# Expert lanes in units of 32 rows, x first in the weights' queue, SSD decays on ScalarE

## The reference

```python
for l in range(DEPTH):
    sh_m, sc_m, g_m, sh_f, sc_f, g_f = split(silu(c) @ w_ada[l] + b_ada[l], 6)
    h = rms_norm(x, norm_gain[l, 0]) * (1 + sc_m) + sh_m
    if l % 2 == 0: y = concat(rwkv7(h @ w_in_even ...), gla(h @ w_in_even ...))
    else:          y = concat(hgrn2(h @ w_in_odd ...), ssd(h @ w_in_odd ...))
    x = x + g_m * (y @ w_out[l])
    h = rms_norm(x, norm_gain[l, 1]) * (1 + sc_f) + sh_f
    x = x + g_f * grouped_moe(h, ...)        # 16 experts, top 2 of one group of 4
return rms_norm(x, final_gain)
```

## Time and profile before

| | us |
|---|---|
| median of 3 runs | 1642.72 |
| lowest, highest | 1634.35, 1645.2 |
| the profiled execution | 1631.18 |
| its span | 1629.4 |

### The profile page before, as it was taken

The page is one execution under the profiler, slowest core; times in us unless marked ns, Lnnn a source line. Parts: engine busy times, 40 slices in busy tenths (PEclk is TensorE's granted clock), DMA queues, the critical chain, the costliest instruction groups (busy, mean ns, idle before and its releaser), DMA issues.

```text
span 1629.4 us, 22551 instructions
## 1 busy us (share of the span) xinstructions
PE 1434.7 (88%) x9837; PEld 743.0 (46%) x9837; DVE 674.6 (41%) x1044; ACT 306.5 (19%) x500; POOL 71.5 (4%) x199
## 2 busy tenths in 40 slices
PE   5999999967878797899999859969998789999992
PEld 3445565536666545433333344535654353333331
DVE  2114334235677316432333235785643543332334
ACT  2121211123342103100000042221112400000002
POOL 7000000000000000000000010000000000000001
PEclk9899999987999898999999979989999989999997
DMA  9686674031000007999997761201100599989884
GB/s 343 219 293 198 207 242 146 1 116 41 3 3 32 24 0 279 404 424 375 353 426 294 273 244 52 78 26 52 52 0 0 233 374 400 386 339 421 335 348 168
DMA packets 91215, 334.17 MB, mean 205 GB/s; under 512 B 6521, under 2 KB 37485, under 8 KB 74733
## 3 DMA queue, kind: packets, MB, share of 16 engines
q1 hardware_dynamic: 76880, 287.94, 46.4%
q10 hardware_dynamic: 8476, 23.82, 3.7%
q0 software_dynamic: 5760, 20.97, 3.4%
HBM read 309.65 MB, written 23.07 MB: 204 GB/s over the span
## 4 chain that ended last, share of the span: by engine, by line
PE 74%; DVE 14%; DMA 6%; ACT 4%; issue 2%; POOL 0%; DVEq 0%; SPq 0%; ACTq 0%; POOLq 0%
PE banks L1736 18%; PE banks L1284 14%; PE banks L1758 10%; PE banks L1656 5%; DVE work L1872 4%; PE banks L1325 4%; PE banks L1273 3%; PE banks L1220 3%; DMA work<-in_w_down_dram 2%; PE banks L1640 2%; PE banks L1719 1%; DVE work L1878 1%; DMA work<-h_rows,idx_tok 1%; PE banks L1450 1%; DMA ring<-in_w_ada_dram 1%
## 5 line engine op out<-in xcount | busy, mean ns | idle before, releaser
L1284 PE MATMUL banks<-h_features,ring 128*128 128x512 f32 (+1 forms) x656 | 291.3, 599 | 5.6 <-ACT h_features L897 4.0
L1736 PE MATMUL banks<-ring,work 128*64 128x512 f32 x672 | 231.3, 600 | 2.3 <-issue 2.3
L1736 PE MATMUL banks<-work 128*64 128x512 f32 x512 | 212.2, 595 | 0.0
L1284 PEld LDWEIGHTS banks<-h_features,ring 128*128 128x128 f32 (+1 forms) x656 | 121.4, 189 | 158.0 <-issue 154.3
L1872 DVE TENSOR_TENSOR work<-work,banks 128x256 f32<-128x256 f32 (+2 forms) x88 | 47.7, 564 | 190.6 <-PE banks L1736 144.7
L1758 PE MATMUL banks<-work 128*64 128x512 f32 x320 | 112.7, 593 | 0.0
L1872 DVE TENSOR_TENSOR work<-work 128x512 f32<-128x512 f32 (+9 forms) x202 | 100.2, 496 | 14.5 <-ACT work L1092 3.6
L1736 PEld LDWEIGHTS banks<-ring,work 128*64 128x64 f32 x672 | 72.1, 138 | 68.6 <-issue 63.9
L1758 PE MATMUL banks<-ring,work 128*64 128x512 f32 x256 | 98.4, 592 | 0.0
L1736 PE MATMUL banks<-h_features,work 128*64 128x512 f32 x192 | 89.5, 614 | 2.2 <-ACT work L1143 2.2
L1656 PE MATMUL banks<-y_features,ring 128*128 128x512 f32 x192 | 84.6, 603 | 6.4 <-DVE small L2404 6.4
(11 more groups left out here) (360 smaller groups left out, 1822.5 us busy)
## 6 DMA issues: line engine op xcount, KB each, us to landing
ring<-in_w_up_dram SPq DMA_DIRECT2D x16, 2048.0 KB, 13.0
y_features<-in_w_ada_dram SPq DMA_DIRECT2D x28, 1024.0 KB, 5.7
work<-in_w_down_dram SPq DMA_DIRECT2D x14, 2048.0 KB, 13.4
ring<-in_w_gate_dram SPq DMA_DIRECT2D x12, 2048.0 KB, 12.2
work<-in_w_up_dram SPq DMA_DIRECT2D x10, 2048.0 KB, 13.3
work<-in_w_gate_dram SPq DMA_DIRECT2D x10, 2048.0 KB, 12.7
ring<-in_w_ada_dram SPq DMA_DIRECT2D x8, 2048.0 KB, 12.2
h_features<-in_w_gate_dram SPq DMA_DIRECT2D x8, 2048.0 KB, 9.4
```

What stands on the lines that cost most here:

```text
L1284: ins = mm(PS[0:w, b, :], lhsT=W[:, k, c0:c0 + w], rhs=h[:, k, :], start=(k == 0), stop=(k == KD - 1))
L1736: ins = mm(PS[rows, bank, :], lhsT=xt[:, k, rows], rhs=ws[lane][:, k, :], start=(k == 0), stop=(k == KD - 1))
```

## The change

Five things:

- **Lanes in units of 32 rows.** `LANES` now counts units of 32 rows, two to a round, and `ROUNDS` is 10. A run may begin or end in the middle of a round: in lane 1 at unit 3 and at unit 11, so rounds 1 and 5 have two experts in that lane. `weights` then returns three parts (rows, weights) instead of two, and `lanes_up` and `lanes_down` loop over them. `choose` takes four numbers for each place (first block, blocks, rows skipped at the front, rows skipped at the end) and puts the rows of an expert accordingly.
- **Start.** SyncE issues x first, then `w_ada[0]` rows in four pairs of row blocks, 2048 columns wide ("first"), the fourth into `y_features`. `first_sums` accumulates them in one bank, quarter g of the columns in part g; one copy and one turn (`first_turn`) replace four.
- **SSD.** The eight subtractions go to ScalarE, as Relu of (cum of the row - value) from PSUM, and the following Exp has scale -1. So does the copy of xs. The decay to the end of the tile is read from the decays themselves (`Es[:, :, P - 1:P]`) instead of being formed apart. `ssd_tile` runs for tiles 0 and 1 before `ssd_scores(0)`.
- **Zeroing.** `lqp` and `lgate` are zeroed for layer 1 by GpSimd after the first layer's combination; VectorE's memsets there go.
- **Order.** The ring order is one entry shorter.

```diff
-LANES = ([1, 1, 1, 1, 2, 1, 2, 2], [2, 3, 2, 1, 2, 1])
-ROUNDS = 11
+QUARTER_ROWS = 32
+LANES = ([2, 2, 6, 2, 2, 4, 2], [3, 3, 2, 3, 3, 4, 2])
+ROUNDS = 10
...
+def place_numbers(u, n, lane):
+    lead = QUARTER_ROWS * (u % 2)
+    skip = -(lead + QUARTER_ROWS * n) % HALF_ROWS
+    return 2 * (u // 2) + lane, (lead + QUARTER_ROWS * n + skip) // HALF_ROWS, lead, skip
...
-    plan = [("ada", 0, i) for i in range(4)]
+    plan = [("first", 0, i) for i in range(3)]
...
+            sp.dma_start(work[:, 0:4096].rearrange("p (a d) -> p a d", d=D),
+                         A["x"][0].rearrange("(a p) d -> p a d", p=P)).then_inc(sem("x_loaded"), 16)
             for n in RING_ORDER:
                 load(n)
+                if n == 2:
+                    sp.dma_start(first_place(3), first_src(3)).then_inc(sem("half_loaded0"), 16)
...
+                if l == 0:
+                    pool.wait_ge(sem("comb_added"), NT)
+                    pool.memset(lqp.rearrange("p a b -> p (a b)"), 0.0).then_inc(sem("pool_const"), 1)
+                    pool.memset(lgate.rearrange("p a b -> p (a b)"), 0.0).then_inc(sem("pool_const"), 1)
...
-                act.wait_ge(sem("seg_diff"), t + 1)
-                act.activation(Es2[t % 2], Es2[t % 2], ACT.Exp).then_inc(sem("seg_exp"), 1)
+                act.wait_ge(sem("score_ready"), 3 * NT + t + 1)
+                for hd in range(8):
+                    ins = act.activation(Es2[t % 2][:, hd, :], PS[:, b + hd // 4, (hd % 4) * P:(hd % 4 + 1) * P], ACT.Relu,
+                                         scale=-1.0, bias=cumc[:, t, hd:hd + 1])
+                link(ins)
+                act.activation(Es2[t % 2], Es2[t % 2], ACT.Exp, scale=-1.0).then_inc(sem("seg_exp"), 1)
...
+            def first_sums(i):
...
+                for k in range(2):
+                    for g in range(4):
+                        ins = mm(PS[32 * g:32 * g + 32, 5, :], lhsT=cond[:, 2 * i + k:2 * i + k + 1].to_broadcast([P, 32]),
+                                 rhs=w[:, k, 512 * g:512 * g + 512], start=(i + k == 0), stop=(i + k == 4))
...
+                    parts = []
                     for lane in range(2):
...
+                        places = [place_at(2 * r + i, lane) for i in range(2)]
+                        width = HALF_ROWS if places[0] == places[1] else QUARTER_ROWS
+                        for i, place in enumerate(places[0:HALF_ROWS // width]):
+                            home = home_of(part, place)
+                            if PLACES[place][0] // 2 == r:
+                                pe.wait_ge(loaded[l][home], 16 * (loads_before(l, home) + loads_of(home, (place, part))))
+                            p0 = HALF_ROWS * lane + QUARTER_ROWS * i
+                            parts.append((slice(p0, p0 + width), home_w(home, part)))
+                    return parts
...
                     for k in ks:
-                        for lane in range(2):
-                            rows = slice(64 * lane, 64 * lane + 64)
-                            ins = mm(PS[rows, bank, :], lhsT=xt[:, k, rows], rhs=ws[lane][:, k, :], start=(k == 0),
+                        for rows, w in ws:
+                            ins = mm(PS[rows, bank, :], lhsT=xt[:, k, rows], rhs=w[:, k, :], start=(k == 0),
                                      stop=(k == KD - 1))
...
+            first_sums(1)
             norm(0)
+            first_sums(2)
+            first_sums(3)
+            first_turn()
             projections(0)
...
                 elif step == LOGS:
-                    signal(dve.memset(f2(lqp), 0.0), "log_pre")
+                    dve.wait_ge(sem("pool_const"), 3)
...
-                for hd in range(8):
-                    link(tsc(Es[:, hd, :], PS[:, b + hd // 4, (hd % 4) * P:(hd % 4 + 1) * P],
-                             cumc[:, t, hd:hd + 1], ALU.subtract, 0.0, ALU.min))
...
-                pk = picked2.rearrange("p k (e n) -> p k e n", n=E)
-                link(tt(pk, bc(at_place, 2, 1), bc(place_of, E, 2), ALU.mult))
+                pk = picked4.rearrange("p k (e n) -> p k e n", n=E)
+                link(tt(pk, bc(at_place, 4, 1), bc(place_of, E, 2), ALU.mult))
                 link(dve.tensor_reduce(begin_runs, pk, AX_X, ALU.add))
...
+                link(tt(late, rank, bc(cap_rows, NT, 1), ALU.is_ge))
+                link(tt(placed, late, bc(skip, NT, 1), ALU.mult))
+                link(tt(placed, placed, rank, ALU.add))
+                link(tt(placed, placed, bc(lead, NT, 1), ALU.add))
```

More of the change, by code:

```diff
@@ L63, in load_plan @@
     at = {phase: i for i, phase in enumerate(phase_order())}
-    loads = sorted((place > 1, at[part, r], lane, at[part, r + n - 1], place, part)
-                   for place, (r, n, lane) in enumerate(places) if r < ROUNDS for part in range(3))
+    loads = sorted((place > 1, at[part, u // 2], lane, at[part, (u + n - 1) // 2], place, part)
+                   for place, (u, n, lane) in enumerate(places) if u < 2 * ROUNDS for part in range(3))
     held = [-1] * 8
@@ L97, in chunk_plan @@
     plan += [("in", 0, i) for i in range(4, 7)]
-    plan += [None, None] + [("out", 0, i) for i in range(2)]
+    plan += [None, None, None] + [("out", 0, i) for i in range(2)]
     plan += [("in", 1, i) for i in range(6)] + [("out", 1, i) for i in range(2)]
@@ L223, in trunk @@
         quarter_ends = small(1)
+        quarter_rows = small(4)
         idx_tok = sb("idx_tok", MAX_BLOCKS + 2, I32)
@@ L438, in trunk, with place_at, home_of, last_home @@
         gathered = [[sem(f"l{l}_{j}_rows_gathered") for j in ("even", "odd")] for l in range(DEPTH)]
-        def home_of(part, r, lane):
-            place = [p for p, run in enumerate(PLACES) if run[2] == lane and run[0] <= r < run[0] + run[1]][0]
+        def place_at(u, lane):
+            return [p for p, run in enumerate(PLACES) if run[2] == lane and run[0] <= u < run[0] + run[1]][0]
+        def home_of(part, place):
             return [home for p, which, home, _ in LOADS if p == place and which == part][0]
+        def last_home(part, lane):
+            return home_of(part, place_at(2 * ROUNDS - 1, lane))
         def loads_of(home, last=None):
@@ L448, in loads_of @@
             return len(users) if last is None else users.index(last) + 1
-        IN_LOOP = [home_of(part, ROUNDS - 1, lane) for part in range(3) for lane in range(2)]
+        IN_LOOP = [last_home(part, lane) for part in range(3) for lane in range(2)]
+        assert len(set(IN_LOOP)) == 6
         loaded = [[sem(f"l{l}_home{i}_loaded" if i in IN_LOOP else f"home{i}_loaded") for i in range(8)]
@@ L561, in units_at @@
             return [("half", HALVES_AT.index((n, i)))] if (n, i) in HALVES_AT else []
-        UNITS = [("piece", i) for i in range(4)] + [unit for n in range(27) for i in range(2) for unit in units_at(n, i)]
-        FIRST_UNITS = 4
-        assert len(UNITS) == 10 + HALVES
+        UNITS = [("first", 0)] + [unit for n in range(27) for i in range(2) for unit in units_at(n, i)]
+        FIRST_UNITS = 1
+        assert len(UNITS) == 7 + HALVES
         def unit_width(unit):
-            return 512 if unit[0] == "piece" else 256
+            return 256 if unit[0] == "half" else 512
         def unit_weights(unit):
@@ L623, in load @@
                     sp.wait_ge(sem("rows_cleared"), 16)
-                if n >= RING and PLAN[n - RING] is not None:
-                    kind, l, i = PLAN[n - RING]
-                    if kind == "ada":
+                earlier = [key for key in PLAN[n % RING:n:RING] if key is not None]
+                if earlier:
+                    kind, l, i = earlier[-1]
+                    if kind == "first":
+                        sp.wait_ge(sem("unit_summed"), i + 1)
+                    elif kind == "ada":
                         sp.wait_ge(sem("unit_summed"), unit_done("piece", i))
@@ L691, in _ @@
                         for lane in range(2):
-                            home = home_of(part, ROUNDS - 1, lane)
+                            home = last_home(part, lane)
                             src = ws[part][l][bass.ds(es[lane], 1)]
@@ L1790, in again @@
                     def again(part):
-                        for home in last[part]:
+                        homes_of = [last_home(part, lane) for lane in range(2)]
+                        for home in homes_of:
                             pe.wait_ge(loaded[l][home], (it + (loads_of(home) + 1)) * 16)
-                        return [home_w(home, part) for home in last[part]]
+                        return [(slice(HALF_ROWS * lane, HALF_ROWS * lane + HALF_ROWS), home_w(home, part))
+                                for lane, home in enumerate(homes_of)]
                     pe.wait_ge(sem(f"l{l}_xt_copied"), it + (ROUNDS + 1))
@@ L2612, in _ @@
             link(dve.memset(lsum, 0.0))
+            parameters()
+            norm(0)
             copy_unit(0)
-            parameters()
-            copy_unit(1)
-            norm(0)
-            for u in range(2, FIRST_UNITS):
```

(1 more changed line is left out.)

174 lines of the change are left out of this document (92 added, 82 removed).

## The result

| | before | after |
|---|---|---|
| median of 4 runs, us | 1643.96 | 1689.01 |
| lowest, highest | 1634.35, 1648.37 | 1686.48, 1692.4 |
| span of the profiled execution | 1629.4 | 1690.6 |

The changed kernel is slower: the ratio of the times is 1.0283, with a 95% interval from 1.0234 to 1.0333. The forecast was 1585.5 with a range from 1564 to 1612; the time lies on the second rival's 1689. Four of the forecast's terms are in the trace nevertheless, so the stages come first.

What follows compares the result with a forecast made beforehand. TensorE was taken as the bound, its long work the expert rounds, with waits at the start and in SSD. Terms -45.2 + 2 + 4 + 2 - 8 - 12 gave -57 us: 1585.5 against the median, range 1564 to 1612.

Steps and rivals of the forecast that it cites:

- the second rival: Mixed steps in rounds 1 and 5 of both layers: widths don't overlap, +46 us in all, 1689 us; chance 0.20.
- Mixed rounds: Rounds 1 and 5 of each layer, 96 steps of three parts: a third part on its own columns nearly free, +2 us.
- the upper end: Mixed rounds, bound from above: 64 to 32 counts as a width change, a step takes 2.00 us for 0.86, +109 us.
- The test at the prediction's end: Expert stages: a mixed round longer than 37 us would above all show the forecast wrong.
- Rounds: Expert stages: 10 static rounds a layer instead of 11, one dynamic pass kept, 2 x 22.6 = -45.2 us.
- Weights: Expert weight transfers: they must fit into one round less, nine loads a layer are tight; 2 us a layer, +4.
- choose(): Table of places on VectorE: about 2.6 us longer, delaying the first loads by the table; +1 us a layer, +2.
- the first rival: Expert weight loads: the transfers bind, the nine tight loads costing 22 us instead of 4, 1603 us; chance 0.16.
- Start: Kernel start: x and row-block pairs load first, projections start near 38.5 for 48.8; -8 us (from -3 to -11).
- the norm needs only x and ends near 34: Start: the norm finishes beside the row-block loads, so the projections' chunk lands last and they start near 38.5.
- 2 us of the gain go back at the lower clock: Start: of the 10 us some 2 return because more of the projections runs at granted clock 0.50.
- SSD: SSD stage: 20 us leave VectorE ahead of the last tile, TensorE's 10.82 us wait shrinks to about 2; -12 us.

Runs made afterwards that it cites:

- e1: The changed kernel, but in mixed rounds both lanes are split, giving four parts of 32 columns and one width per step: 1584.4 us, ratio to before 0.9657.
- e3: The kernel before, with only lane 1 of rounds 1 and 5 of each layer worked in two 32-wide parts with the same weights: 1747.51 us, ratio 1.0661.
- e2: The changed kernel, but each run of steps in a mixed round works its 32-wide parts first, then its 64-wide ones: 1668.66 us, ratio to before 1.0191.
- e4: The kernel before, with both lanes of all 11 static rounds worked in four 32-wide parts with the same weights: 1640.94 us, ratio 1.000.
- e5: The changed kernel with the experts of before (11 static rounds, 64-row units), leaving the start and the decays: 1623.05 us, ratio to before 0.9904.
- e6: e1 with one change of order at the start, the norm's sums before the second pair of row blocks: 1583.72 us, ratio to before 0.9663.

## Why the prediction was wrong, point by point

**Mixed rounds** (taken at +2, bounded by +109): this is the step that failed. The rows gave 109 for the upper end, the runs 105 to 107: 105 from after to e1, 106.6 in e3. The place was as forecast, but a mixed step, taken to cost 0.02 us more, costs 1.11. The upper bound was built from the right rows, the late weight load of 0.52 us and the first pass of 0.48, and it even had the period, 2.00 us for 1.98. What went wrong is the choice between the ends. I argued that the change in the earlier trace rows was between widths that share columns, while the parts of a mixed step share none, and that pairs and fours start together. But each of those pairs and fours is of one width. The only rows with two widths in sequence showed a weight load that waited for the change, and no row showed two widths together. e3 shows that separate columns don't help. The rule of the Trainium skill that the prediction set beside them (TensorEngine Tiling (Array Packing), Key Properties: changing the tiling mode drains TensorE) makes no exception for them. The trace agrees, with 0.13 us a change and 0.86 us of lost overlap a step in e2. This rival deserved more than 0.20. The test at the prediction's end, a mixed round above 37 us, has come out against it: 22.6 and the 27.2 more make 49.8 us.

**Rounds** (-45.2): right, 22 reciprocals and rounds of 22.6 us. **Weights** (+4) and **choose()** (+2): e1 shows them without the mixed steps. Its two expert stages are 19.3 and 19.0 us shorter than before, 38.3 together; the forecast's own terms without start and SSD make 45.2 - 2 - 4 - 2 = 37.2. In layer 0 the first gate product of round 1 starts 51.0 us behind the router's first matmul (680.97 - 629.93) for 48.9 before (673.99 - 625.10): 2.1 us for the table and its first loads, where I had 1. But this place moves between executions: 48.9 to 51.0 us in the four runs with the old choose() (before, e3, e4, e5), 51.0 to 52.6 in the four with the new one. The means are 2 us apart, and under 1 in layer 1, so the forecast's 1 a layer is about right. TensorE's waits in e1 for transfers that were not so before (view of the waits, layer 0; total, times, longest):

```profile
PE banks L1809 <- DMA y_features<-in_w_gate_dram: 1.3, 1, 1.3
...
PE banks L1809 <- DMA h_features<-in_w_up_dram: 0.6, 1, 0.6
```

From 680.97 on the layer is then 21.5 us shorter, 1.1 short of 22.6, where I had left 2; in layer 1 it is 2.2 short. So the first rival is out: with no slack from slow mixed rounds, the tight loads arrive in time but for such short waits. The prediction's 54 transfers a layer were miscounted: the plan has 42, and the dynamic loop's pass 6 more. Nothing in the sum was made from the 54.

**Start** (-8): the projections start 5.4 us earlier, not 10. The step "the norm needs only x and ends near 34" overlooked the order of TensorE's list; e6 shows it. The other half, that 2 us of the gain go back at the lower clock, doesn't show either. The granted clock between 40 and 45 is 0.50 in after, as before, but from the first projection to the modulation's next sums the same 36 records take no longer than before. The windows, first of before, then of after (columns as in rows 3):

```profile
48.76:64.84 16.08, 16.08 (x36) 6.83 (x40) 1.84 (x8) 4.88 (x8) 0.00 (x0) 0.87 0.74 229
43.31:58.89 15.58, 15.58 (x36) 6.69 (x40) 1.83 (x8) 4.88 (x8) 3.32 (x33) 0.90 1.03 336
```

**SSD** (-12): the wait before the last tile is 3.3 us for 10.82 (after, waits of TensorE from 1060 to 1140):

```profile
PE banks L1679 <- DVE work L1945: 3.3, 1, 3.3
```

Until the product behind that tile (line 1273 at 1117.49, line 1341 at 1143.11) the stage is 12.2 us shorter, as forecast, though not in the forecast's parts (10.6 for the wait, 2 for the clock, less 0.6). The wait gave 7.5. From the tile to that product it is 16.2 us for 18.9, so 2.7 came back with the clock (0.99 for 0.89, window below). The other 2.0 lie ahead of the wait. That the parts make up the same sum is partly luck. By the output projection it is 9.5; in e1, e2 and e5 the same stretch is 7.7 to 10.6 shorter. The difference arises behind that product: from there to the output projection it is 133.6 us in before, e2, e3, e4 and e6 and 136.3 to 136.6 in after, e1 and e5, whatever the code. ScalarE's eight activations cost what the rows of before had said, 2.2 us a tile; the timeline of ScalarE in after, start us and us for the eight together:

```profile
1077.55 2.17 ACT L1138 ACTIVATE work<-banks,work 128x128 f32<-128x128 f32 x8 [1.36 <-DVE work L2429]
```

The Trainium skill (ScalarE: Activation LUTs, Rules for kernel authors) would have relu on VectorE, by a ratio that it gives for bf16. The data here are float32, and this trace shows no gain that it would bring: 2.17 us a tile on an engine that is 19% busy, where eight of VectorE's subtractions took 2.8. The first window of after covers the work that leads up to that tile: TensorE is busy for 7.55 of 10.80 us and the clock at 1.00, where before TensorE stood still and the clock was at 0.63. The second begins with the tile, as the second of rows 12 does:

```profile
1116.00:1126.80 10.80, 7.55 (x25) 3.20 (x21) 9.38 (x17) 4.84 (x7) 0.00 (x0) 1.00 0.00 0
1126.80:1153.20 26.40, 23.10 (x128) 14.92 (x128) 18.12 (x25) 4.01 (x6) 0.00 (x0) 0.99 0.23 80
```

**Sum.** With the mixed rounds at their measured price the forecast's other terms give 1585.5 - 2 + 106 = 1689.5, and 1689.01 was measured; without any price 1583.5, and e1 measured 1584.4. That the two fit so well is partly chance: start and SSD together gave 2 (e5) to 5 us (the stages) less than forecast, and the median of the runs of before moved by 3.5 us from set to set (1643.96, 1640.91, 1640.42).

## What to carry to other kernels

Before a tile of TensorE is cut in a new width, look whether every other part that runs beside it has that width. If not, price it as two groups one behind the other, and cut the neighbours too: four parts of one width cost what two cost (e4), three parts of two widths cost more than double (e3). When a bound from rows is at hand and only an argument speaks for the other end, the argument needs a row of its own. And a transfer that is moved forward gains nothing until the consumer's list has been read for what stands ahead of it.

## What the runs showed of the hardware that was not expected

- A change between 32 and 64 columns costs 0.13 us where groups of four steps alternate (e2), and takes the overlap of parts on separate columns with it: 1.97 us a step for 0.86 (after, e3).
- Twice the matmul and weight-load records of half the width take the same 22.60 us a round (e4).
- The stage from the first projection to the router of layer 0 differs between executions of the same code. Ahead of the experts e3 and e4 are the kernel before. The chain of waits of e3 has its router at

```profile
635.31 5.98 PE banks L1665 x16
```

and that of e4 at

```profile
633.49 6.02 PE banks L1665 x16
```

where it was 625.10. From the first projection it takes 586.3 and 582.5 us in them, 576.3 in before. The granted clock between 364 and 561 is 0.87 and 0.89 in them, 0.92 in the profiled execution of before. The 8.5 us that after lost in this stage lie within that spread and can't be charged to the change; 586.36 in e1 and 574.5 in e6 (614.55 - 40.03), which run the same code there, show the same spread. What sets the clock's falls in that stage stays open.
